# Last norm: GpSimd multiplies by the weights, VectorE only scales; the last expert's slots are split by column halves

## The reference, cut to what matters

```
def rms_norm(x, gain):
    xf = x.astype(jnp.float32)
    inv = lax.rsqrt(jnp.mean(xf * xf, axis=-1, keepdims=True) + NORM_EPS)
    return (xf * inv * gain.astype(jnp.float32)).astype(x.dtype)
...
        xin = h[bidx, idx]                       # 64 tokens of each expert
        ...
        out = zeros.at[bidx, idx].add(contrib)   # scatter of the experts' rows
...
        x = x + merged @ w_out[layer]
    return rms_norm(x, final_gain)
```

## Time and profile before

| | us |
|---|---|
| median of 3 runs | 1468.22 |
| lowest and highest | 1467.8 and 1468.32 |
| the profiled execution, its own time | 1466.85 |
| its span in the trace | 1465.0 |
| VectorE busy in it | 547.6 |
| ScalarE busy in it | 340.0 |
| GpSimd busy in it | 114.5 |

### The profile page before, as it was taken

How to read it: one execution, slowest core, us unless ns; L and a number is a source line. 1 busy time by engine, 2 the same in 40 slices (tenths; PEclk the granted TensorE clock), 3 DMA queues, 4 the chain that set the end, 5 groups by cost and what they waited for, 6 DMA issues and landing times.

```text
span 1465.0 us, 16663 instructions
## 1 busy us (share of the span) xinstructions
PE 1373.4 (94%) x6713; PEld 737.6 (50%) x6713; DVE 547.6 (37%) x967; ACT 340.0 (23%) x549; POOL 114.5 (8%) x188
## 2 busy tenths in 40 slices
PE   7999999999998898998988988989999999999997
PEld 6778533333333232332322323323378787888876
DVE  7675621121211121121111211113278587756663
ACT  5893110010000010010000100103042465533322
POOL 0000000000000000000000000002022215550000
PEclk9999999999999999999999999999999999999999
DMA  9149899999999999999999999999975132353221
GB/s 324 22 168 390 329 421 405 429 428 429 429 429 429 429 429 429 429 429 429 429 429 429 429 427 429 429 428 428 420 242 132 58 105 83 83 173 133 94 107 58
DMA packets 67875, 467.05 MB, mean 319 GB/s; under 512 B 5744, under 2 KB 30576, under 8 KB 42608
## 3 DMA queue, kind: packets, MB, share of 16 engines
q1 hardware_dynamic: 63008, 454.71, 75.4%
q0 software_dynamic: 4528, 11.18, 3.1%
q10 hardware_dynamic: 288, 0.45, 0.1%
HBM read 458.22 MB, written 7.05 MB: 318 GB/s over the span
## 4 chain that ended last, share of the span: by engine, by line
PE 62%; DMA 30%; DVE 4%; ACT 2%; issue 2%; DVEq 0%; POOL 0%; ACTq 0%
DMA wide<-in_w_up 21%; PE bank L1035 13%; PE bank L975 12%; PE bank L727 8%; PE bank L728 8%; PE bank L729 8%; DMA early<-in_w_up 8%; PE bank L914 4%; PE bank L1005 1%; PE bank L1073 1%; DVE nrm L1749 1%; PE bank L1132 1%; PE bank L1160 1%; PE bank L757 1%; PE bank L762 0%
## 5 line engine op out<-in xcount | busy, mean ns | idle before, releaser
L975 PE MATMUL bank<-wide,xinT 128*64 128x512 f32 x1376 | 307.0, 596 | 41.9 <-DMA wide<-in_w_up 24.4
L975 PEld LDWEIGHTS bank<-wide,xinT 128*64 128x64 f32 x1376 | 96.6, 137 | 248.1 <-issue 170.8
L975 PE MATMUL bank<-early,xinT 128*64 128x512 f32 x656 | 147.0, 595 | 19.4 <-DMA early<-in_w_up 10.7
L1749 DVE SCALAR_TENSOR_TENSOR th<-th,bank 128x512 f32<-128x512 f32 x32 | 20.6, 684 | 385.2 <-ACT th L1458 385.2
L1035 PE MATMUL bank<-wide,actT 128*64 128x512 f32 x656 | 144.9, 594 | 3.6 <-issue 3.5
L727 PE MATMUL bank<-hT_lo,ring_r 128*128 128x512 f32 x352 | 138.6, 394 | 1.4 <-ACT gt L1323 1.1
L729 PE MATMUL bank<-hT_hi,ring_r 128*128 128x512 f32 x352 | 137.1, 390 | 0.0
L728 PE MATMUL bank<-hT_hi,ring_r 128*128 128x512 f32 x352 | 137.0, 389 | 0.0
L1458 ACT ACTIVATE th<-bank 128x512 f32<-128x512 f32 x32 | 17.4, 594 | 475.3 <-PE bank L975 475.3
L1746 DVE TENSOR_TENSOR ring_r<-ring,ring_r 128x2048 fp32r<-128x2048 f32 (+1 forms) x40 | 89.5, 2237 | 59.6 <-ACT ring_r L1291 59.2
L975 PEld LDWEIGHTS bank<-early,xinT 128*64 128x64 f32 x656 | 46.0, 137 | 118.5 <-issue 79.5
(11 more groups left out here) (427 smaller groups left out, 1705.7 us busy)
## 6 DMA issues: line engine op xcount, KB each, us to landing
wide<-in_w_gate SPq DMA_DIRECT2D x43, 2048.0 KB, 37.6
wide<-in_w_up SPq DMA_DIRECT2D x42, 2048.0 KB, 38.0
wide<-in_w_down SPq DMA_DIRECT2D x38, 2048.0 KB, 38.4
early<-in_w_down SPq DMA_DIRECT2D x21, 2048.0 KB, 38.5
early<-in_w_up SPq DMA_DIRECT2D x21, 2048.0 KB, 38.3
early<-in_w_gate SPq DMA_DIRECT2D x20, 2048.0 KB, 39.9
ring<-in_w_in SPq DMA_DIRECT2D x25, 1024.0 KB, 6.2
ring<-in_w_out SPq DMA_DIRECT2D x8, 1024.0 KB, 4.9
```

What stands on the lines that cost most here:

```text
L975: last = pe.matmul(bank[1 + 2 * (m % 2) + q // 2][o:o + 64, :], xinT[:, k, :], w[:, i, q * 512:(q + 1) * 512], start=(k == 0), stop=(k == ...
L1749: return dve.scalar_tensor_tensor(out_, a, s, b, op0, op1)
```

## The change

It does two things. In the last norm GpSimd multiplies each merged half by its weights into another memory, `hT`, while ScalarE squares the same half; what VectorE has left is to scale the product by the row's number, an instruction with one tensor input. GpSimd's small addition of eps stands between the products. Each scaling waits for its product (`weighted`). In the slots, `slot_hi` and `slot_lo` are each made in two halves of 256 columns, with a count of their own, and TensorE waits for each half; its low matmuls follow four steps behind the high ones.

```
@@ TensorE
-                    lead = 5
-                    pe.wait_ge(slot_high, 1)
+                    lead = 4
                     for step in range(KT + lead):
-                        if step == lead:
-                            pe.wait_ge(slot_low, 1)
-                        for slots, at in ((slot_hi, step), (slot_lo, step - lead)):
+                        for slots, there, at in ((slot_hi, slot_high, step), (slot_lo, slot_low, step - lead)):
                             if 0 <= at < KT:
                                 k = Y_ORDER[at]
+                                if at % 4 == 0:
+                                    pe.wait_ge(there, at // 4 + 1)
@@ ScalarE
-            act_e.activation(slot_hi, th[:, 0, :], ACT.Copy, scale=stat[:, 50:51]).then_inc(slot_high, 1)
+            for h in range(2):
+                hs = slice(256 * h, 256 * h + 256)
+                act_e.activation(slot_hi[:, hs], th[:, 0, hs], ACT.Copy, scale=stat[:, 50:51]).then_inc(slot_high, 1)
@@ GpSimd
-            for t in range(TT):
-                c = stat[:, 48 + t:49 + t]
-                pool.wait_ge(square_sum, 2 * TT + 2 * t + 1)
-                pool.tensor_scalar(c, stat[:, 40 + 2 * t:41 + 2 * t], 1.0, EPS, ALU.mult, ALU.add).then_inc(half_sum, 1)
+            pool.wait_ge(gfin_in, 16)
+            for o in range(2 * TT):
+                t, h = o // 2, slice(o % 2 * 512, o % 2 * 512 + 512)
+                if o % 2:
+                    pool.wait_ge(square_sum, 2 * TT + o)
+                    pool.tensor_scalar(stat[:, 48 + t:49 + t], stat[:, 39 + o:40 + o], 1.0, EPS, ALU.mult,
+                                       ALU.add).then_inc(half_sum, 1)
+                was_read(pool, f"fin{o}")
+                pool.tensor_tensor(hT[:, o, :], added[:, t, h], gfin[:, h], ALU.mult).then_inc(weighted, 1)
@@ VectorE
-            dve.wait_ge(slot_high, 1)
             dve.wait_ge(slot_gained, 1)
-            stt(slot_lo, th[:, 0, :], stat[:, 50:51], slot_hi, ALU.mult, ALU.subtract).then_inc(slot_low, 1)
+            for h in range(2):
+                hs = slice(256 * h, 256 * h + 256)
+                dve.wait_ge(slot_high, h + 1)
+                stt(slot_lo[:, hs], th[:, 0, hs], stat[:, 50:51], slot_hi[:, hs], ALU.mult, ALU.subtract).then_inc(slot_low, 1)
@@ VectorE, finished
-                    r = added[:, t, 512 * h:512 * h + 512]
-                    stt(r, r, stat[:, 52 + t:53 + t], gfin[:, 512 * h:512 * h + 512], ALU.mult,
-                        ALU.mult).then_inc(final_ready, 1)
+                    dve.wait_ge(weighted, 2 * t + h + 1)
+                    dve.tensor_scalar(added[:, t, 512 * h:512 * h + 512], hT[:, 2 * t + h, :], stat[:, 52 + t:53 + t], None,
+                                      ALU.mult).then_inc(final_ready, 1)
```

More of the change, by code:

```diff
@@ L355, in build @@
         eps_set, deviation = sem("eps_set"), sem("deviation")
+        weighted = sem("weighted")
         gf_half_in, pairs_ready, slot_sums, slot_gained = (
```

## The result

| | median us (runs) | lowest to highest | span of the profiled execution | its own time |
|---|---|---|---|---|
| before | 1468.22 (9) | 1465.81 to 1469.25 | 1465.0 | 1466.85 |
| after | 1471.57 (9) | 1470.45 to 1473.03 | 1468.9 | 1470.71 |

The ratio is 1.0025, with a 95% interval of 1.0017 to 1.0034. The kernel is slower by some 3.4 us, where the forecast had 2.8; the time lies in the range and 0.6 us above the forecast.

What follows compares the result with a forecast made beforehand. TensorE is busy 94% of the span, but GpSimd's last instruction and its drain were taken to set the end. Tail +2.6 and slots +0.18 gave 1468.22 + 2.8 = 1471.0 us, range 1467.6 to 1472.5.

Steps and rivals of the forecast that it cites:

- The program's end: Tail: GpSimd's drain ends 7.2 us behind its last instruction and sets the end; that instruction moves +2.6 us.
- The first rival: Program's end: GpSimd's drain isn't bound to its last instruction, the end goes with the outputs; 1468.6 or 1467.9 us; 20%.
- the variant that counts the drain from the issue of the last product: Program's end: the drain's 7.43 us count from the last product's issue; +1.6 + 0.18, 1470.0 us.
- The slots: Split of slot_hi and slot_lo: ScalarE's two instructions delay the weight unit and first projection matmul by 0.18 us.
- The exclusion: Last norm: VectorE's scalings and GpSimd's products exclude each other in turn; last product ends between 1460.2 and 1460.5.
- The third rival's no exclusion: Last norm: scalings and products don't exclude each other but the drain follows; last product at 1459.33, 1470.1 us; 20%.
- GpSimd's own pace: Last norm: two products and the eps addition take 2.79 us, against 2.80 for two merges.
- The rival on the slower side: Last norm: GpSimd wins each time it meets VectorE; +3.8 + 0.18, 1472.2 us; 25%.
- Its deciding place: At 1452.4: if product 3 precedes the first scaling, that scaling ends at 1454.05 and the next merge is 0.9 us late.
- The sum: Whole kernel: +2.6 us in the tail and +0.18 at the slots, median 1471.0 us, 0.19% more.
- that class: Total time: slower by over 0.2% (2.9 us), given 36%: the 25% case and a third of the forecast's own 35%.
- the outputs: End of the last norm: the last two scalings end at about 1460.9 and 1461.2, 0.2 us later than before.

Runs made afterwards that it cites:

- scale_on_scalar: The kernel after the change, but ScalarE makes the eight scalings and VectorE only merges and takes reciprocals; 1469.58 us in one run.
- scalings_last: The kernel after the change, but VectorE does all eight scalings behind the last merge, none between merges; 1470.29 us in one run.
- late_small: The kernel before, plus one unread 128x1 GpSimd addition that waits until all outputs are computed; 1471.89 us, ratio 1.0031.
- shared_tail: The kernel before, with the last norm's products and scalings shared among GpSimd, ScalarE and VectorE, ScalarE issuing the last output; 1467.75 us, ratio 1.0002.
- eps_on_scalar: The kernel before, with the last norm's eps additions moved from GpSimd to ScalarE; 1466.85 us, ratio 0.9993.

## Why the prediction was right, and the term that was mis-sized

**The program's end.** The step on which the forecast stood, that GpSimd's last instruction and 7.2 us of drain set the end, held. The drain ends 7.20 us behind that instruction in the kernel before, after the change, in both halves of it, in `scale_on_scalar` and in `scalings_last`, and 7.18 us behind it in `late_small`, which shows it by adding that instruction alone. The first rival (20%) is out. So is the variant that counts the drain from the issue of the last product: the record starts 2.29 us before the product's end instead of 0.23, and lasts 2.05 us longer.

**The slots.** Forecast +0.18, measured +0.18, in the whole change and alone. It is made as the prediction had it: after the change ScalarE's two instructions end at 1067.92 + 0.91, and the copy behind them begins 0.82 us behind the first of them, where it was 0.63.

```profile
1067.92 0.91 ACT L1484 ACTIVATE slot_hi<-th,stat 128x256 fp32r<-128x256 f32 x2 [0.30 <-POOL stat L1657]
1068.74 1.04 ACT L1485 ACTIVATE ring_r<-ring 128x1024 fp32r<-128x1024 f32 x1
```

VectorE's first half of the low part of the weight unit, which had waited 0.20 us for that copy, now waits 0.39, and starts 2.47 us behind GpSimd's factor instead of 2.29:

```profile
1069.81 1.23 DVE L1753 TENSOR_TENSOR ring_r<-ring,ring_r 128x1024 fp32r<-128x1024 f32 x1 [0.39 <-ACT ring_r L1485]
```

What the split was for did happen and was worth nothing: TensorE's last slot matmul ends 3.40 us behind the factor instead of 3.77, but TensorE then only waits longer for the projection, 1.11 us instead of 0.55.

**The exclusion.** Held. The prediction took it from VectorE's instructions with two SBUF inputs; the scaling has one, and is excluded as well. It takes 0.49 us when it starts shortly before a product's end and up to 1.19 when it starts earlier in one, and each of the long ones ends 0.28 or 0.29 us behind that product; three of GpSimd's eight products took 1.39 to 1.49 us, the others 1.30 or 1.31. The Trainium skill (SBUF — State Buffer, section "SBUF: two separate sides") has the lock taken by an instruction in a 2-port mode as by one with two SBUF inputs; the trace agrees, with 1.19 us where 0.49 is normal; in which mode the scaling runs no row says. The third rival's no exclusion (20%) is out.

**GpSimd's own pace: the term that was mis-sized.** The prediction made two products and an addition 2.79 us, just below two merges (2.80), by summing durations. A pair comes every 2.89 to 2.92 us even with nobody in its way (`scale_on_scalar`), since 0.08 to 0.09 us lie ahead of each addition and as much behind it, though what they wait for is there. It isn't the wait as such: from the first product of a pair to the second, which has its own wait, there is no gap, it starts 0.04 us before the other's end. What makes the gaps stays open. GpSimd therefore falls behind the merges, and its last product no longer waits for the last merge: free of exclusion it ends at F + 2.83, where the prediction had 1459.33 - 1457.19 = 2.14. Most of these 0.69 us are the gaps: eight of them, 0.67 us, less 0.13 for the three overlaps. The rest is the start: from the first product's, F - 8.82, eight products and four additions come to F + 2.29 even by their durations alone. With exclusion it said 3.0 to 3.3 and it is 3.53; the exclusion's own price was put too high (0.9 to 1.2, measured 0.70), so the two errors partly cancel. The last merge is 0.49 us late for this reason, not 0.14: product 5 begins late enough (1456.96) to hold scaling 3 until 1458.54.

**The rival on the slower side (25%), GpSimd first each time they meet.** Its deciding place went to VectorE: the first scaling takes 0.49 us and the merge behind it starts at 1453.78, when its bank is there, not 0.9 us late. The two didn't meet there as the prediction had it: GpSimd was late, product 2 ended at 1453.35, and product 3 came at 1453.79, when the scaling was over. The point from which it was to decide, a last product behind 1460.4, F + 3.2, was passed all the same (F + 3.53), by the slower pace. So this number didn't tell the two cases apart as the prediction said it would; the duration of the first scaling did.

**The sum.** Forecast +2.6 for the tail and +0.18; in the traces +3.12 and +0.18, 3.3 us, and 3.35 between the medians. The profiled spans differ by 3.9 only because of the 0.60 us of spread ahead of the slots. That the sum came so near has some luck in it: the pace was put too low by 0.69 us and the exclusion too high by 0.2 to 0.5. That the result lies over the bound of 0.2% (2.9 us) and the forecast under it comes from the 0.5 us by which the tail was mis-sized. The chance for that class had a third of the forecast's own case in it, with the reason that it ended 0.1 us short of the bound.

**What it was worth to the outputs.** The prediction had them 0.2 us later; VectorE ends at F + 4.21 instead of F + 3.77, 0.44 later, and SP's drain ends at F + 6.73 instead of 6.04. So even with no drain of GpSimd in the way the change would have lost 0.7 us against the kernel before, an estimate from the last two numbers.

## What to carry to other kernels

Look at the last instruction of every engine, and not only at the chain of waits that ends in the output: here an engine with 8% of the span in busy time set the end, by an addition of one column, through a drain that stands in the list of the program's end and in no chain. Move work off GpSimd in the last microseconds rather than onto it, unless the last transfer lands later than GpSimd's last instruction and its drain. When an engine is to run at the pace of another, read its gaps from the trace too: here a sum of durations at 99.6% of the period (2.79 of 2.80 us) was 0.1 us over it. And when work moves to another queue, follow it to the last transfer: `shared_tail` took GpSimd out of the way and lost by its squares, which then stood behind scalings, and by its last outputs.

## What the hardware showed that I had not expected

- GpSimd's drain at the program's end takes 7.2 us behind its last instruction with 99 DMAs issued by GpSimd in the program, 8.42 with 131 and 8.75 with 195. VectorE's ends 0.05 us behind its last instruction in the kernel before, SP's lasts 0.007 us.
- The drain starts to count at the end of the last instruction, whatever its kind: 7.20 behind a product of 1.39 us, 7.18 behind an addition of 0.19. Where GpSimd's last instruction is the issue of a DMA, it ends 10.6 us behind it (1324.25 to 1334.87, `eps_on_scalar`), and 10.8 in the same kernel once more.
- An addition of one column on GpSimd takes 0.18 or 0.19 us, and 0.25 to 0.27 next to VectorE's scalings after the change.
- On GpSimd 0.08 to 0.09 us lie between a product of 128x512 and an addition of one column, in either order, even where nothing is left to wait for; between two such products there is no gap, whether or not VectorE works beside them.
